# Expert products in chunks of 64 slots, in both column halves of the array, from fp32 weights as loaded

## The reference, cut to what matters

```python
flat_e = e_idx.reshape(-1)             # 1280 (token, expert) pairs
order = jnp.argsort(flat_e)
tok = order // TOP_K
sizes = jnp.bincount(flat_e, length=N_EXPERTS)
xs = t[tok]
hid = silu(ragged_dot(xs, w_gate, sizes)) * ragged_dot(xs, w_up, sizes)
y = ragged_dot(hid, w_down, sizes)
y = y * gate.reshape(-1)[order][:, None]
return zeros((B * L, D)).at[tok].add(y)
```

## Time and profile before

| | |
|---|---|
| median of three runs | 2076.99 us |
| the profiled execution, its own time | 2079.55 us |
| its span | 2077.8 us |
| PE busy | 1763.5 us (85%) |
| DVE busy | 1296.8 us (62%) |
| ACT busy | 961.8 us (46%) |
| POOL busy | 209.0 us (10%) |
| bytes moved by DMA | 376.64 MB |
| mean granted TensorE clock | 0.929 |

### The profile page before, as it was taken

One profiled execution on the slowest core, in us unless ns is written; L12 is line 12 of the kernel. 1 busy time (PEld: TensorE's weight loads), 2 busy tenths in 40 slices (PEclk: granted clock), 3 DMA queues, 4 the chain that ended last, 5 costly groups with the idle time before them and its releaser, 6 DMA issues. The chain is left out here.

```text
span 2077.8 us, 40338 instructions
## 1 busy us (share of the span) xinstructions
PE 1763.5 (85%) x15365; PEld 1455.0 (70%) x15366; DVE 1296.8 (62%) x1885; ACT 961.8 (46%) x1490; POOL 209.0 (10%) x267
## 2 busy tenths in 40 slices
PE   3998879899696799999919988899986939999992
PEld 0898678788454588888818986788873527888882
DVE  2388255556445696896663883556662368999674
ACT  2244523233312786786432454333332138888651
POOL 0000022222000100000020001212220010000001
PEclk7999999999797899999959999999997969999996
DMA  7221093420313798897643111331004059999854
GB/s 313 71 82 44 31 358 126 154 102 2 107 59 152 285 384 340 335 401 286 228 153 98 55 44 51 127 125 52 3 2 145 31 209 385 397 398 397 355 199 165
DMA packets 112110, 376.64 MB, mean 181 GB/s; under 512 B 14730, under 2 KB 35490, under 8 KB 86374
## 3 DMA queue, kind: packets, MB, share of 16 engines
q1 hardware_dynamic: 83310, 303.85, 39.2%
q10 hardware_dynamic: 20168, 39.89, 5.0%
q0 software_dynamic: 8496, 30.94, 4.0%
HBM read 332.87 MB, written 41.78 MB: 180 GB/s over the span
## 5 line engine op out<-in xcount | busy, mean ns | idle before, releaser
L1955 DVE TENSOR_TENSOR expert_w_lo<-shared,expert_w_hi 128x2048 fp32r<-128x2048 f32 x192 | 430.6, 2285 | 44.6 <-ACT expert_w_hi L1897 44.3
L1897 ACT ACTIVATE expert_w_hi<-shared 128x2048 fp32r<-128x2048 f32 x192 | 360.6, 1915 | 42.4 <-PEq L141 37.8
L1839 PE MATMUL ps<-expert_w_hi,expert_x_hi 128*128 128x512 f32 x592 | 232.3, 392 | 5.1 <-DVE expert_x_lo L1951 5.1
L1840 PE MATMUL ps<-expert_w_lo,expert_x_hi 128*128 128x512 f32 x592 | 232.0, 392 | 0.0
L1841 PE MATMUL ps<-expert_w_hi,expert_x_lo 128*128 128x512 f32 x592 | 232.0, 392 | 0.0
L1839 PEld LDWEIGHTS ps<-expert_w_hi,expert_x_hi 128*128 128x128 f32 x592 | 112.2, 190 | 29.3 <-issue 5.9
L1841 PEld LDWEIGHTS ps<-expert_w_hi,expert_x_lo 128*128 128x128 f32 x592 | 112.1, 189 | 23.5
L1840 PEld LDWEIGHTS ps<-expert_w_lo,expert_x_hi 128*128 128x128 f32 x592 | 112.1, 189 | 23.2
L1875 PE MATMUL ps<-expert_w_hi,expert_hid_hi 128*128 128x512 f32 x296 | 118.5, 400 | 2.2 <-ACT expert_hid_hi L1929 1.2
L1011 POOL TENSOR_TENSOR mixer_NTb<-mixer_Bt,consts_sb 128x256 f32<-128x256 f32 x120 | 88.4, 760 | 286.3 <-DVE mixer_Bt L1286 222.7
L1876 PE MATMUL ps<-expert_w_lo,expert_hid_hi 128*128 128x512 f32 x296 | 115.4, 390 | 0.0
(11 more groups left out here) (344 smaller groups left out, 3741.1 us busy)
## 6 DMA issues: line engine op xcount, KB each, us to landing
shared<-in_w_gate SPq DMA_DIRECT2D x64, 1024.0 KB, 7.1
shared<-in_w_up SPq DMA_DIRECT2D x64, 1024.0 KB, 8.7
shared<-in_w_down SPq DMA_DIRECT2D x64, 1024.0 KB, 9.0
qkv<-in_w_ada SPq DMA_DIRECT2D x20, 1280.0 KB, 6.0
shared<-in_w_in SPq DMA_DIRECT2D x10, 2048.0 KB, 7.8
y_table<-expert_y ACTq DMA_DIRECT2D x37, 512.0 KB, 8.8
qkvT<-in_w_ada SPq DMA_DIRECT2D x20, 768.0 KB, 8.4
y_table<-zero ACTq DMA_DIRECT2D x1, 12800.0 KB, 50.9
```

The costliest lines, as they stand in the source:

```text
L1839: pe.matmul(bank, hi, w_hi[:, j, w], start=first, stop=False)
L1840: pe.matmul(bank, hi, w_lo[:, j, w], start=False, stop=False)
L1897: act.activation(w_hi[:, j, :], raw[:, j, :], ACT.Copy).then_inc(w_hi_done, 1)
L1955: dve.tensor_tensor(w_lo[:, j, :], raw[:, j, :], w_hi[:, j, :].bitcast(F32), ALU.subtract).then_inc(w_lo_done, 1)
```

## The change

- A chunk has CH = 64 slots. The routing tables, `h_table`'s gather (64 rows) and `y_table` (MAXC = 35 chunks of 64 rows, 9.2 MB instead of 13.1 MB) follow, and the loop over further chunks has NF - 1 = 9 iterations.
- No operand is split: PE multiplies plain fp32. The stationary operand is 64 slots wide. Each product is made twice per k-step, once for each half of the output's columns, the first into partitions 0 to 63 of the bank and the second into 64 to 127. Gate and up have 256 moving columns per instruction, down 512, and all of down lies in one bank.
- The hidden rows lie as 128 partitions x 256 and are turned by ordinary products with a 64x64 unit matrix, one for each half (eight instructions per half of the hidden columns).
- There are two weight sets: even experts use `raw`, odd ones `odd_weights`. The loop over experts runs over pairs. The pieces of expert e + 2 are loaded when expert e's last chunk has used them (`used`), expert 1's at the start of the phase.
- On PE the eight transposes of the next chunk all stand ahead of the turns of the hidden rows. DVE copies both `xT` and `hidT`; ACT copies y and issues two stores of 128 KB, one for each half.

```diff
-MAXC = 2 * T // P + NE - 1
+CH = 64
+NF = T // CH
+MAXC = 2 * T // CH + NE - 1
...
                 with eng.If(n > 1):
-                    with eng.Fori(0, NT - 1) as c:
+                    with eng.Fori(0, NF - 1) as c:
                         with eng.If(n > c + 1):
-                            chunk(e, nc.s_assert_within(base + c, 0, MAXC - 1), False, final)
+                            chunk(i, s, nc.s_assert_within(base + c, 0, MAXC - 1), False, final)
...
+            with eng.Fori(0, NE // 2 - 1) as i:
+                expert(i, 0, False)
+                expert(i, 1, False)
+            expert(NE // 2 - 1, 0, False)
+            expert(NE // 2 - 1, 1, True)
...
+                for j in range(PIECES):
+                    sp.sem_inc(w_in[0][j], 16)
+                    sp.dma_start(odd[:, j, :], piece_of(A, l, 1, j)).then_inc(w_in[1][j], 16)
+                with sp.Fori(0, NE // 2 - 1) as i:
+                    for s in range(2):
+                        for j in range(PIECES):
+                            sp.wait_ge(used[s][j], i + 1)
+                            sp.dma_start(w[s][:, j, :], piece_of(A, l, i * 2 + (2 + s), j)).then_inc(w_in[s][j], 16)
...
+                def turn(k):
+                    pe.wait_ge(gathered, k * 16 + 16)
+                    pe.sem_inc(passed, 1)
+                    for n in range(KD):
+                        tr = pe.transpose(turned[:, n * CH:(n + 1) * CH], xg[:, n:D:KD], G.c("ident")[0:CH, 0:CH])
+                    tr.then_inc(xt_p, 1)
                 def hid_turn(k, m):
                     pe.wait_ge(hid_done, k * 2 + (m + 2))
+                    pe.sem_inc(passed, 1)
                     for n in range(HQ):
-                        q = m * HQ + n
-                        tr = pe.transpose(hid_turned(m)[:, n * P:(n + 1) * P], hid[:, q:FF:KF], G.c("ident"))
+                        for r in range(2):
+                            tr = pe.matmul(hid_turned(m)[half(r), n * CH:(n + 1) * CH], hid[half(r), m * HQ + n:FH:KF],
+                                           G.c("eye")[half(r), :], start=True, stop=True)
                     tr.then_inc(ht_p, 1)
...
+                            for r in range(2):
+                                mm = pe.matmul(G.ps[half(r), n, 0:FH], xT[:, q * CH:(q + 1) * CH],
+                                               w[s][:, j, at + r * FH:at + (r + 1) * FH], start=(q == 0), stop=(q == KD - 1))
                             if last and q == 3:
-                                mm.then_inc(half_used, 1)
+                                mm.then_inc(used[s][2 * n], 1)
                         mm.then_inc(done, 1)
-                    turn(k + 1, 0, 4)
+                    turn(k + 1)
                     hid_turn(k, 0)
-                    turn(k + 1, 4, 6)
                     hid_turn(k, 1)
-                    turn(k + 1, 6, KD)
...
+                        for r in range(2):
+                            mm = pe.matmul(G.ps[half(r), 5, :], hT[:, q * CH:(q + 1) * CH], w[s][:, j, at + r * OH:at + (r + 1) * OH],
+                                           start=(q == 0), stop=(q == KF - 1))
...
+                    act.activation(sg[:, :], G.ps[:, 0, 0:FH], ACT.Silu).then_inc(sg_done, 1)
+                    act.wait_ge(y_p, k + 2)
...
+                    act.activation(y[:, :], G.ps[:, 5, :], ACT.Copy).then_inc(y_done, 1)
+                    act.wait_ge(y_done, k + 2)
...
+                    for r in range(2):
+                        act.dma_start(dst[:, r * OH:(r + 1) * OH], y[half(r), :]).then_inc(y_out, 16)
...
                     for m in range(2):
+                        dve.wait_ge(ht_p, k * 2 + (m + 2))
+                        dve.tensor_copy(hT[:, m * HQ * CH:(m + 1) * HQ * CH], hid_turned(m)).then_inc(hT_done, 1)
                     take(k + 1)
```

More of the change, by code:

```diff
@@ L85, in constants @@
                                 np.broadcast_to(np.arange(P)[:, None], (P, NT))], axis=2).reshape(P, 2 * NT)
-    parts["places"] = np.broadcast_to(i, (P, P))
-    parts["bounds"] = np.broadcast_to(np.arange(MAXC + 1)[None, :] * P, (P, MAXC + 1))
-    parts["floors"] = np.broadcast_to(np.array([-1] + [c * P for c in range(1, NT)])[None, :], (P, NT))
+    parts["places"] = np.broadcast_to(i[:, 0:CH], (P, CH))
+    parts["bounds"] = np.broadcast_to(np.arange(MAXC + 1)[None, :] * CH, (P, MAXC + 1))
+    parts["floors"] = np.broadcast_to(np.array([-1] + [c * CH for c in range(1, NF)])[None, :], (P, NF))
     pos = np.arange(DEC_SEQ)
@@ L1871, in chunk @@
                         if q % HQ == 0:
[L1872 to L1878, removed]
@@ L1890, in _ @@
             def _(act):
-                def take(k):
-                    act.wait_ge(xt_p, k + 2)
-                    act.wait_ge(u_p, k + 1)
-                    act.activation(x_hi[:, :], turned, ACT.Copy).then_inc(x_hi_done, 1)
-                def split(j):
-                    act.activation(w_hi[:, j, :], raw[:, j, :], ACT.Copy).then_inc(w_hi_done, 1)
-                act.sem_inc(ya, 1)
-                act.sem_inc(y_out, 16)
-                split(0)
-                act.wait_ge(xt_p, 2)
@@ L1903, in _ @@
-                act.activation(x_hi[:, :], turned, ACT.Copy).then_inc(x_hi_done, 1)
-                for j in range(1, PIECES):
-                    split(j)
-                def chunk(e, k, last, final):
-                    def next_hi(j):
-                        if last and not final:
-                            act.wait_ge(raw_in[j], e * 16 + 16)
-                            if j % 2 == 0:
-                                act.wait_ge(half_used, e * 3 + (j // 2 + 1))
-                            elif j < 5:
-                                act.wait_ge((g_p, u_p)[j // 2], k + (1 + j // 2))
-                            else:
-                                act.wait_ge(y_p, k * 2 + 3)
-                            split(j)
+                act.sem_inc(y_out, 32)
@@ L1920, in chunk @@
+                def chunk(i, s, k, last, final):
                     act.activation(warm[:, :], G.eps[:, :], ACT.Silu)
                     act.wait_ge(g_p, k + 1)
+                    if last:
+                        act.sem_inc(used[s][1], 1)
                     act.wait_ge(hid_done, k * 2 + 1)
-                    act.activation(sg[:, :], G.ps[:, 0, :], ACT.Silu).then_inc(sg_done, 1)
-                    for j in range(3):
-                        next_hi(j)
-                    act.wait_ge(y_p, k * 2 + 1)
@@ L1927, in chunk @@
-                    for m in range(2):
-                        act.wait_ge(ht_p, k * 2 + (m + 2))
-                        act.activation(h_hi[:, m * HQ * P:(m + 1) * HQ * P], hid_turned(m), ACT.Copy).then_inc(h_hi_done, 1)
-                    take(k + 1)
-                    next_hi(3)
-                    next_hi(4)
-                    act.wait_ge(y_p, k * 2 + 3)
-                    act.wait_ge(y_out, k * 16 + 16)
-                    act.activation(y[:, 0:512], G.ps[:, 5, :], ACT.Copy).then_inc(ya, 1)
@@ L1959, in _ @@
-                split(0, 0)
-                take(0)
-                for j in range(1, PIECES):
-                    split(0, j)
-                def chunk(e, k, last, final):
-                    def next_lo(j):
-                        if last and not final:
-                            split(e + 1, j)
-                    next_lo(0)
+                    dve.wait_ge(xt_p, k + 2)
+                    dve.wait_ge(u_p, k + 1)
+                    dve.tensor_copy(xT[:, :], turned).then_inc(xT_done, 1)
```

160 lines of the change are left out of this document (62 added, 98 removed).

## The result

Four runs of the changed kernel gave 2229.18 to 2236.12 us, a median of 2234.78, beside 2076.16 for the kernel before on the same chip. The ratio is 1.076 with a 95% interval of 1.074 to 1.0781: slower by 158.6 us. The direction was forecast, the time (2103, 2064 to 2155) was not. The profiled span grows from 2077.8 to 2232.8 us, by 155.0.

The account below looks back on a forecast made before the run. PE's instruction stream bounds the expert phases: 57 chunks of 12.3 us (701), plus 10 control flow, 4 half clock, minus 1, make 714 against 688.1 us, so 2103 us for the kernel, range 2064 to 2155.

Parts of the forecast that it names:

- The products: Gate/up and down on PE: column halves overlap nearly fully, 64 x 0.108 + 16 x 0.215 = 10.35 us a chunk.
- D: Rival: the two column halves run one after the other, 590 us more, 2690 us; chance 0.03.
- The turn-around: From a chunk's last up product to its first down product: 1.9 us, bounds 1.5 and 2.3.
- The control flow: Skipped iterations of the further-chunk loop: 0.3 us each, 10 us late on PE in all, bounds 0 and 45.
- The clock: Half clock at the start of each expert phase: 4 us in all.
- The sum: Both expert phases: 701 + 10 + 4 - 1 = 714 us against 688.1, +26 us.
- B: Rival: turn-around 1.5 us and control flow hidden, period 11.8 us, 12 us less than before, 2065 us; chance 0.22.
- G: Rival: the edge between B and the main forecast, a chunk period of 12.0 to 12.1 us, no change; chance 0.10.
- C: Rival: paired halves run at the 128-column rows' rate or weight loads show between them, 48 us more, 2150; chance 0.11.
- E: Rival: DMA binds in single-chunk experts, 56 us more at most, up to 2160 us; chance 0.06.
- F: Rival: PE's larger loop code must be read again, 100 us or more, 2200 us; chance 0.05.
- My own sign: Whole kernel slower, chance 0.68; wrong in sign if the chunk period is below 12.0 us.

Follow-up runs that it names:

- e7_split: Changed kernel with n - 1 loops, the eight transposes split five and three around the first hidden turn: 2130.02 us, ratio 1.0261 to the kernel before.
- e5_five: Changed kernel with a loop of 5 instead of 9 iterations over further chunks: 2137.15 us, ratio 1.0312 to the kernel before.
- e1_two: Changed kernel with a loop of 2 instead of 9 iterations over further chunks: 2116.61 us, ratio 1.0195 to the kernel before.
- e4_dyn: Changed kernel with the further-chunk loop running exactly n - 1 times, no condition inside: 2116.31 us, ratio 1.0185 to the kernel before.

## Why the prediction was right, and where it was wrong

- **The products** were right in kind: the halves run together at 0.110 us per 256-column instruction (0.108 taken, 0.117 the upper end) and 0.216 per 512 columns (0.215). The prediction's D, serial halves, is refuted. The 0.002 over 64 instructions is 0.13 us a chunk.
- **The turn-around** was mis-sized: 2.20 us against 1.9. Of my terms the transposes took 1.03 instead of 0.9, the first hidden turn 0.73 instead of 0.5, copy and hand-over 0.44 as worked out. The changes of tiling, which I had put in the bounds, are in the stream: e7_split prices two further ones at 0.1 us each. The Trainium skill's rule on a change of tiling mode ("TensorEngine Tiling (Array Packing)", Key Properties), by which the turn-around would be nearer 2.3, was closer than my sum. Both terms make the period 12.70 instead of 12.3, 23 us over 57 chunks.
- **The control flow** is the step that failed. It was taken as 10 us with an upper bound of 45 and cost 82.9. The prediction read a border's control from ACT, 2.13 us with three skips, let "PE's sequencer" have "the same to do", and priced a skip at 0.3: 3.6 us against 2.9 of cover. The cover was right, 2.95 us. The need was not: PE takes 7.25 us, 0.74 for each of eight skips and 1.3 for the rest, and it takes 3.67 with three skips where ACT took 2.13. A skip is dearer on PE than on ACT (0.74 against 0.44), and even ACT's price was over the 0.3 taken. So 15 x (7.25 - 2.95) + 5 x (6.51 - 2.95) gives 82.3, and the longer first one nearly all of the rest. The upper bound fell with it: it too rested on ACT's rows, which bound neither PE's skip nor its 1.3. The Trainium skill ("Advanced Engine Details and Errata", Control Flow Timing) would make a skip at least 0.16 us by its two figures, an estimate; the runs show more than four times that, and they decide.
- **The clock** was left out behind the stalls. The prediction had 4 us for the starts of the phases and no term for a drop in mid-phase; it is some 43 us in all. Gaps of 3.4 to 4.5 us cost it (0.60 granted behind them), gaps of 1.1 to 1.4 us don't (1.00 in e5_five). This is a step missing, not a number off, and the fault is that a stall was priced at its own length.
- **The sum** was 714 us for the phases: 23 more for the period, 73 for the control flow, 39 for the clock and 1 for the start make the 849.9 measured. The turn-around and the products alone would have left the time inside my range; control flow and clock, 112 us, took it out.
- **The rivals.** B (period 11.8) and G (12.0) are out: the period is 12.70 without any stall, and e1_two, which has none, is still 2% slower than before. C lies between: the pair rate lost 0.002, not 0.009. E is out, no PE row waits for weights, although the DMA share is 1.01 in single-chunk experts. F is out: the instruction reads rise from 103 to 111 only, none of them falls between 742.4 and 1050.7 us of the span while the gaps recur there, and e4_dyn lost nothing to its equal code. My own sign held for the reason named, a period over 12.0: without the stalls (e1_two) the time is still 40 us over before. It is 13.6 us above my 2103, of which 10 were for a control flow that e1_two doesn't pay.

That 57 periods of 12.70 (724) stand against 37 of 18.26 (676) is 48 us, of which the shorter stretch between the phases gives some back; 40 remain without skips. PE's stream of products alone, 10.5 us of the 12.70, leaves 1.5 for everything else before the change could break even, and the chain over DVE alone takes 1.8. I found no order that gets there. Giving one-chunk experts the 64-slot form and the others the old one would win a period of 12.70 for 18.26 twelve times, but the old form's single weight buffer is filled at a DMA share of 1.01 exactly there, and 17.0 us of transfer an expert leave little; it was not tried.

## What to carry to other kernels

A loop with a fixed trip count around a condition is priced in skipped iterations on the engine that sets the time. Look whether its next work is already late at the present count, because how much cover is left can't be read from the absence of a gap, and read the price on that engine's own records, not on another's. Use the trip count itself as the bound. Price a stall on TensorE with the clock behind it: here 4 us of rest cost 1.7 us more, and up to 3.0. And halving a chunk halves only the columns' work: what is paid per chunk (here 2.2 of 12.7 us) is then paid half as often again.

## What the runs showed of the hardware

- A skipped iteration (a compare-and-branch for the condition, another back to the head) costs PE 0.74 us, in both kernels; DVE 0.54, ACT 0.44.
- Column halves overlap almost fully when alternated (0.110 us per instruction of 256 columns). In blocks of 16 instructions they stand 0.216 apart, and only some four on either side of a change of half still overlap (0.180 on average).
- Going once more from transposes of 64 rows to quadrant products and back cost PE about 0.2 us, 0.1 a change.
- Gaps of 0.3 to 1.4 us on PE left the granted clock at 1.00; gaps of 3.4 to 4.5 us were followed by some 3 us mostly at the lower level (0.60 over 4.2 us).
